# Key norms of the recurrent mixers: one transpose and two transfers in place of spreading products

## What is computed

```python
w_log = -jax.nn.softplus(-(w0 + jnp.tanh(wd) @ w_w2).astype(f32)) - 0.5
decay = jnp.exp(-jnp.exp(w_log))
a = jax.nn.sigmoid((a0 + ad @ w_a2).astype(f32))
kk = (k * k_k).reshape(B, T, RWKV_HEADS, HEAD_DIM)
kk = kk / jnp.maximum(jnp.linalg.norm(kk, axis=-1, keepdims=True), 1e-12)
k = k * (1.0 + (a - 1.0) * k_a)
...
s_kk = jnp.einsum('bhvk,bhk->bhv', S, kk_t)
S = (S * w_t[:, :, None, :] - s_kk[..., None] * (kk_t * a_t)[:, :, None, :]
     + v_t[..., None] * k_t[:, :, None, :])
...
bonus = jnp.sum(r * k * r_k, axis=-1, keepdims=True) * v
```

## Time and profile before

| | |
|---|---|
| median of 3 runs | 2789.36 us (2786.97 to 2793.34) |
| the profiled execution | 2792.05 us, of which 2790.3 us are its span |
| TensorE products, busy share of the span | 96% |
| VectorE, ScalarE, GpSimd | 53%, 35%, 7% |
| mean granted clock of TensorE | 0.98 |

### The profile page before, as it was taken

The page is one execution under the profiler, slowest core; times in us unless marked ns, Lnnn a source line. Parts: engine busy times, 40 slices in busy tenths (PEclk is TensorE's granted clock), DMA queues, the critical chain, the costliest instruction groups (busy, mean ns, idle before and its releaser), DMA issues.

```text
span 2790.3 us, 42160 instructions
## 1 busy us (share of the span) xinstructions
PE 2690.6 (96%) x17668; PEld 2212.2 (79%) x17668; DVE 1489.0 (53%) x1850; ACT 965.1 (35%) x1472; POOL 206.2 (7%) x284
## 2 busy tenths in 40 slices
PE   6999999999999999999999999999999999978998
PEld 5888878787888887888877787888878777768787
DVE  6555575765565434333356754333355565775644
ACT  3222233623222233222335433222233544533332
POOL 3000000220000000000000410000000000043000
PEclk9999999999999999999999999999999999988999
DMA  7566552102556322233222102232233331240222
GB/s 296 188 215 218 172 187 91 65 3 98 211 192 223 126 95 89 86 103 105 83 91 79 33 32 83 89 107 90 91 101 127 104 106 68 87 116 4 69 94 76
DMA packets 53370, 313.41 MB, mean 112 GB/s; under 512 B 7617, under 2 KB 7745, under 8 KB 24929
## 3 DMA queue, kind: packets, MB, share of 16 engines
q1 hardware_dynamic: 41760, 236.65, 24.9%
q0 software_dynamic: 11456, 74.55, 7.9%
HBM read 302.69 MB, written 2.20 MB: 109 GB/s over the span
## 4 chain that ended last, share of the span: by engine, by line
PE 91%; DVE 5%; DMA 2%; ACT 1%; issue 1%; POOL 0%; SPq 0%; DVEq 0%; ACTq 0%
PE ps L971 18%; PE ps L972 18%; PE ps L973 18%; PE ps L1259 6%; PE ps L1260 6%; PE ps L1261 6%; PE ps L2130 1%; PE ps L2114 1%; PE ps L2127 1%; PE ps L1526 1%; PE ps L1528 1%; PE ps L1527 1%; DMA ada_first<-in_ada 1%; DVE w_lo L947 1%; PE ps L1341 1%; PE ps L1996 1%
## 5 line engine op out<-in xcount | busy, mean ns | idle before, releaser
L971 PE MATMUL ps<-hn_hi,w_hi 128*128 128x512 f32 x1440 | 564.9, 392 | 16.6 <-DVE hn_lo L920 16.6
L972 PE MATMUL ps<-hn_lo,w_hi 128*128 128x512 f32 x1440 | 563.9, 392 | 0.0
L973 PE MATMUL ps<-hn_hi,w_lo 128*128 128x512 f32 x1440 | 563.8, 392 | 0.0
L947 DVE TENSOR_TENSOR w_lo<-w_raw,w_hi 128x2048 fp32r<-128x2048 f32 (+2 forms) x227 | 467.9, 2061 | 163.0 <-ACT w_hi L940 162.9
L940 ACT ACTIVATE w_hi<-w_raw 128x2048 fp32r<-128x2048 f32 (+2 forms) x227 | 390.7, 1721 | 94.0 <-PE ps L1261 90.6
L971 PEld LDWEIGHTS ps<-hn_hi,w_hi 128*128 128x128 f32 x1440 | 272.8, 189 | 75.5 <-issue 18.4
L1259 PE MATMUL ps<-hn_hi,w_hi 128*128 128x512 f32 x776 | 316.3, 408 | 15.6 <-DVE spare L1454 7.0
L972 PEld LDWEIGHTS ps<-hn_lo,w_hi 128*128 128x128 f32 x1440 | 272.8, 189 | 56.8
L973 PEld LDWEIGHTS ps<-hn_hi,w_lo 128*128 128x128 f32 x1440 | 272.5, 189 | 56.9
L1260 PE MATMUL ps<-hn_lo,w_hi 128*128 128x512 f32 x776 | 307.8, 397 | 0.0
L1261 PE MATMUL ps<-hn_hi,w_lo 128*128 128x512 f32 x776 | 307.3, 396 | 0.0
(11 more groups left out here) (461 smaller groups left out, 3518.3 us busy)
## 6 DMA issues: line engine op xcount, KB each, us to landing
w_raw<-in_up SPq DMA_DIRECT2D x88, 1024.0 KB, 4.8
ada_w<-in_ada POOLq DMA_DIRECT2D x64, 1024.0 KB, 5.1
w_raw<-in_down SPq DMA_DIRECT2D x64, 704.0 KB, 4.1
w_raw<-in_mix_in SPq DMA_DIRECT2D x20, 1024.0 KB, 4.8
w_raw<-in_dsa_in SPq DMA_DIRECT2D x18, 1024.0 KB, 5.2
w_raw<-in_merge SPq DMA_DIRECT2D x16, 768.0 KB, 4.2
ada_first<-in_ada SPq DMA_DIRECT2D x8, 1024.0 KB, 12.3
w_raw<-in_mix_out SPq DMA_DIRECT2D x8, 1024.0 KB, 4.9
```

The source lines that it names most:

```text
L947: dve.tensor_tensor(w_lo[:, slot, 0:size], w_raw[:, slot, 0:size], w_hi[:, slot, 0:size].bitcast(F32), ALU.subtract).then_inc(w_lo_ready, 1)
L971: pe.matmul(bank, wh, x_hi[:, k], start=(k == 0), stop=False)
L972: pe.matmul(bank, wh, x_lo[:, k], start=False, stop=False)
L973: return pe.matmul(bank, wl, x_hi[:, k], start=False, stop=(k == K - 1))
```

## The change

The two groups of spreading products and the VectorE products that read them are replaced. TensorE transposes the 128 x 16 reciprocals once into PSUM; VectorE copies the 16 x 128 result into a corner of `rw_bonus`; SP, which waits for that copy, writes it to device memory (8 KB) and reads it back twice, each time sent to the 64 partitions of one head of each pair, into the whole of `rw_bonus` (2 x 256 KB). This stands in SP's program behind the `lora` load. VectorE makes `k * k_k * rw_r` in two instructions, and multiplies with the spread reciprocals behind `rw_kk`. As `rw_bonus` is in use until then, the bonus products move behind the factors.

```diff
+        kk_rows = nc.dram_tensor("kk_rows", (16, P), F32, kind="Internal").ap()
...
+        def kk_spread_sp(sp, l):
+
+            sp.wait_ge(kk_norms, 2 * l + 2)
+            sp.dma_start(kk_rows[:], rw_bonus[0:16, 0, 0:P]).then_inc(kk_spread, 16)
+            sp.wait_ge(kk_spread, 48 * l + 16)
+            rows = kk_rows[:].rearrange("(j n h) t -> h j n t", j=2, h=2).rearrange("h j n t -> h (j n) t")
+            for hp in range(2):
+                sp.dma_start(rw_bonus[half(hp)].rearrange("p j (n t) -> p (j n) t", t=P),
+                             rows[hp:hp + 1].broadcast_to([HD, 2 * NB, P])).then_inc(kk_spread, 16)
...
                 if kind == "mix_in":
                     sp.wait_ge(piece_done, p0 + 1)
                     sp.dma_start(lora[:], w["lora"][:, at[0]]).then_inc(lora_loaded, 16)
+                    kk_spread_sp(sp, at[0])
...
             if at == 16:
                 pe.wait_ge(kk_norms, 2 * l + 1)
-                head_spread_pe(pe, 7, 0).then_inc(kk_spread, 1)
-            if at == 17:
-                pe.wait_ge(kk_norms, 2 * l + 2)
-                head_spread_pe(pe, 7, 1).then_inc(kk_spread, 1)
+                pe.transpose(ps[0:16, 7, P:2 * P], head_roots[:].rearrange("p j n h -> p (j n h)"), ident[:]).then_inc(kk_turned, 1)
...
-                if at in (17, 18):
-                    j = at - 17
-                    dve.wait_ge(kk_spread, 2 * l + j + 1)
-                    last = dve.scalar_tensor_tensor(rw_a[:, j], k[:, j], vcol(l, "k_k", j), ps[:, 7], ALU.mult, ALU.mult)
-                    last.then_inc(kk_raw if j else kk_norms, 1)
                 if at == 17:
+                    dve.wait_ge(kk_turned, v)
+                    dve.tensor_copy(rw_bonus[0:16, 0, 0:P], ps[0:16, 7, P:2 * P]).then_inc(kk_norms, 1)
                     dve.wait_ge(gates_ready, 4 * l + 1)
...
             dve.wait_ge(gates_ready, 4 * l + 2)
-            dve.wait_ge(kk_raw, v)
-            own(dve.tensor_tensor(rw_a[:], rw_a[:], rw_r[:], ALU.mult))
+            for j in range(2):
+                own(dve.scalar_tensor_tensor(rw_a[:, j], k[:, j], vcol(l, "k_k", j), rw_r[:, j], ALU.mult, ALU.mult))
             dve.wait_ge(gates_ready, 4 * l + 3)
             own(dve.tensor_tensor(rw_kk[:], rw_kk[:], k, ALU.mult))
-            for j in range(2):
-                last = dve.scalar_tensor_tensor(rw_bonus[:, j], r[:, j], vcol(l, "r_k", j), rw_kk[:, j], ALU.mult, ALU.mult)
-            last.then_inc(bonus_raw, 1)
+            dve.wait_ge(kk_spread, 48 * v)
+            own(dve.tensor_tensor(rw_a[:], rw_a[:], rw_bonus[:], ALU.mult))
             dve.wait_ge(decays_ready, v)
...
             dve.tensor_tensor(rw_ki[:], rw_kk[:], rw_ki[:], ALU.mult).then_inc(factors_ready, 1)
+            for j in range(2):
+                last = dve.scalar_tensor_tensor(rw_bonus[:, j], r[:, j], vcol(l, "r_k", j), rw_kk[:, j], ALU.mult, ALU.mult)
+            last.then_inc(bonus_raw, 1)
```

More of the change, by code:

```diff
@@ L393, in program @@
         kk_norms = sem("kk_norms")
-        kk_raw = sem("kk_raw")
+        kk_turned = sem("kk_turned")
         kk_spread = sem("kk_spread")
```

## The result

| | before | after |
|---|---|---|
| median of 7 runs each | 2791.97 us (2786.97 to 2793.42) | 2800.42 us (2793.39 to 2802.97) |
| ratio after / before | | 1.0030 (1.0020 to 1.0041) |
| span of the profiled execution | 2790.3 us | 2798.3 us |
| first mask behind the reciprocal, layer 0 and 1 | 30.11, 30.11 us | 32.96, 33.96 us |

The account below looks back on a forecast made before the run. TensorE stands on 91% of the chain, but it and VectorE end almost together before the recurrence's mask. Two layers of 3.25 us plus 0.75 for the clock add 8.0 us, to 2797.4 us; range 2792.5 to 2804.0.

Parts of the forecast that it names:

- TensorE's relief: Layer's projection: TensorE ends 1.9 us earlier, the piece ScalarE waits for 1.0 us earlier; alone this gains almost nothing.
- SP's order: SP's queue: mix_out's first weights wait behind copy, write and spreads, landing at 548.15, so ScalarE's split starts 3.45 us later.
- both bounds: Landing of SP's write to device memory: between 2.0 us (64 KB partition swaps) and 2.6 us (output stores); 2.3 taken.
- the sum: One layer, ScalarE's split to first mask: 3.45 later start, -0.68, -0.84, +1.41, -0.1, giving 3.25 us; clock adds 0.75.
- From the split to the mask: ScalarE's split near 548.2 to mask near 567.0: ScalarE decides, VectorE hides with 0.3 us to spare; bonus pair adds 1.41.
- The clock: TensorE idles 3.25 us before the factors; its clock falls to 0.50 over first products and bonus sum, costing 0.75 us a layer.
- The total: Whole kernel: two layers of 3.25 + 0.75 us, 8.0 us slower, 2797.4 us; chance 0.56.
- Small runs cheap (1): Spreads: small runs cheap, clock stays up, weights land at 546.95 to 547.3; +4 to +5 us, 2793.9; chance 0.20.
- Not slower (2): Weights land before 543.7, ahead of ScalarE's need; mask -0.6 to +0.2 us a layer, 2788 to 2789.8; chance 0.08.
- The clock that stays low (3): Recurrence: clock stays low, or spreads take 99 ns a run; +11 to +16 us, 2803 as middle; chance 0.12.

Follow-up runs that it names:

- e1: Changed kernel with SP issuing the first two mix_out weight loads ahead of its wait, the write and the spreads; ratio to the kernel before 1.0024.
- c2: e1 with state clears moved early, norms spread into rw_bi and multiplied before the last split, bonus products ahead of the decays again; ratio to the kernel before 1.0006.
- e4: Kernel before with one wait added: SP waits for the key norms' first product before the mix_out loads, no new transfers; ratio 1.0001.
- the second execution: Changed kernel profiled once more, unedited; reciprocal to first mask 33.39 and 33.30 us in layers 0 and 1.
- e6: Changed kernel with the first mix_out weight load issued between the write of the reciprocals and the two spreads; one execution, 2802.09 us.
- e5: Changed kernel with reciprocals stored head by head, so spreads read runs of 4 KB instead of 512 bytes; ratio to the kernel before 1.0028.
- e7: e1 with two more TensorE products that nothing reads, behind the first bonus sum; ratio to the kernel before 1.0010.

## Why the prediction was right, and where it wasn't

**TensorE's relief, and that it is worth nothing by itself: right.** The piece that ScalarE's split waits for was done 1.0 us sooner (its wait was 4.49 us in e1, 5.50 before), the end of the projection 2.0 us sooner (in c2 561.72 - 1.62 = 560.10, 26.6 us behind the reciprocal, against 562.33, 28.65 behind it); forecast were 1.0 and 1.9. No version turned that into a shorter kernel (in c2 the mask came 0.35 us sooner, but the ratio is 1.0006).

**SP's order: right in kind, with two sizes off that nearly cancel.** The copy (0.28 us, 4.5 us behind the reciprocal) and the write's issue came as worked out. The write landed in 1.4 us, below both bounds, where 2.3 stood in the sum, so the load was issued 7.67 us behind the reciprocal and not 8.32. The spreads began to move about 1.5 us after their issue where a load's 0.95 stood, and moved for about 2.6 us by the DMA share in layer 0 (540.6 to 543.2), with 2.5 in the sum. With the sum's 3.15 and 0.65 behind them the load lands at 547.0, and the split began at 547.06: in that layer the parts are right. But from the load's issue to the split it took 6.55, 7.93, 7.27 and 7.28 us in the four layers seen, 6.2 in the sum, so three of them are 0.7 to 1.4 us above the first. No step of mine has this. The second weight load, which in the kernel before has to wait until 531.96, follows here 0.67 us behind the first and landed 8.3 us after its issue; but it follows as closely in e4, and there the first lands after 4.8 us, as alone. So a second load behind it isn't enough to delay the first, and what does, behind the spreads, stays open. The split came 14.2, 15.5, 14.9 and 14.8 us behind the reciprocal; forecast 14.5.

**From the split to the mask: right in size, half right in its reason.** 18.84 us forecast; 18.74, 18.47, 18.46 and 18.46 measured. The bonus pair took the 1.41 us and L2798 the 1.41 that the rows without GpSimd gave. I had ScalarE decide, with 0.3 us to spare on VectorE. In layer 0 of the first profile VectorE decided: its split took 3.33 us and rw_kk 2.00 where I had 2.29 and 1.6 (the two new products took 1.96, not 2.8), and it reached the decays 0.4 us behind the last exponential; in the second execution ScalarE decided by 0.48. The two are that close.

**The clock: fell where I said, cost nothing there.** Granted 0.50 from 563 to 566, as forecast. But the sum had it low through the bonus sum, whose end it put at 570.6, 7.05 us behind the factors. It was back at 0.88 in 566 to 567 and at 1.00 behind that: the first products took 4.0 us and not 4.8, the bonus sum 1.12 and not 2.2, and it ended at 568.05, 5.07 us behind the factors. The first products that the mask reads were done when VectorE had got through the bonus pair and the convolution, and the first level began 2.79 us behind the mask (568.59 - 565.80), exactly as before, half a microsecond behind the bonus sum's end. The 0.75 us a layer in the sum was 0: the term had the low clock last too long.

**The total: 8.0 against 8.0, partly by luck.** Two layers of masks brought 2.85 + 3.85 = 6.7 us (in the second execution 3.28 + 3.19 = 6.5), against 6.5 without the clock's term. But up to 2599 only 5.3 us of them had come through; the fall at 2610 adds 3.2, and no step of mine had it (in the second execution, 8.2 up to there and 11.5 behind it). It stands where the sum had 1.5 us for a clock that cost nothing. So the mechanism of SP's queue was right and its size near; that the totals agree to a tenth is luck, and the interval, 5.6 to 11.4 us, wouldn't show a miss of two.

**The rivals.** Small runs cheap (1): the runs' length made no difference that can be told, and the load came no sooner. Not slower (2): e1 is that case, weights in time, and e6 nearly, and the mask is at +0.10 us, inside the -0.6 to +0.2 worked out. The time isn't: 1.0024, 6.7 us, because the price left out the clock in the levels, 4.3 us for two layers; in e1's profile 3.3 more came with the fall at 2610. So rival 2 was wrong where it ended near zero; had SP's order been kind, the change would still have been slower. The clock that stays low (3) didn't come in the changed kernel's two profiles; in layer 1 of e5, the same order of work, it did fall in the levels, at a cost that can't be told.

## What to carry to other kernels

A transfer put into an in-order queue is paid for by the loads behind it: look up what they feed, and when they are due, not only when the transfer itself is wanted; a wait ahead of them can be free (23 us of it were here) and half a megabyte not. Time taken from an engine that isn't last in that stretch becomes idle time, and where short dependent steps follow, the idle time can lower TensorE's clock and cost more than was saved; so ask where a new gap would lie, ahead of covered work or ahead of the chain. A gap ahead of covered work isn't safe by that: in c2 and in layer 1 of e5 the first products behind it ran at the full clock, and the fall came in the levels. Moving work between a producer and its consumer's next step (the bonus pair) opens such a gap even if the work itself takes as long as before.

## What the runs showed of the hardware

- More work on TensorE made the kernel faster: 1.88 us of products that nothing reads kept the granted clock at 1.00 and took 5.7 us off two recurrences (e7 against e1; 3.9 by the ratios). Over all kernels, mask to split in both layers together was 139.3 to 145.2 us where the clock fell in the levels of both layers and 134.4 to 136.4 in the others.
- A fall of the clock to 0.50 cost nothing that shows in the changed kernel, where it lay over covered products (563 to 566), and about 2 us a layer in e1, where it lay over the levels and lasted longer (570 to 574).
- A spread of 256 KB landed 3.8 us after its issue with runs of 512 bytes (4.3 in the second execution) and with runs of 4 KB.
- Of two loads of 1 MB issued 0.37 us apart, with nothing ahead of them, the first landed after 4.8 us, as alone (e4).
- Eight products of 128 columns took 1.16 us, sixteen of 64 columns 1.09.
- A pair of VectorE instructions of one form took 2.41 us beside GpSimd (c2) and 1.41 without it (L2803).
